# Paged samples: score before weighing, key gathers in groups of four, keys transposed by head pair

## The reference, cut to what matters

```
z      = q . k / 8 + bias[head]
log_1m = log_sigmoid(-z)                       # softplus(z), negated
rest   = sum of log_1m over all keys later than k
a      = exp(log_sigmoid(z) + rest)
out    = sum over k of a * v
```

## Time and profile before

| | us |
|---|---|
| median of three runs | 3324.55 |
| lowest, highest | 3321.88, 3334.59 |
| the profiled execution | 3332.23 |
| its span in the trace | 3330.1 |
| 32 steps of the changed stage, first exp to last exp | 1922.1 to 2677.0 |

### The profile page before, as it was taken

One profiled execution on the slowest core, in us unless ns is written; L12 is line 12 of the kernel. 1 busy time (PEld: TensorE's weight loads), 2 busy tenths in 40 slices (PEclk: granted clock), 3 DMA queues, 4 the chain that ended last, 5 costly groups with the idle time before them and its releaser, 6 DMA issues. The chain is left out here.

```text
span 3330.1 us, 47096 instructions
## 1 busy us (share of the span) xinstructions
PE 2939.2 (88%) x17542; PEld 2124.0 (64%) x17542; DVE 1658.2 (50%) x2730; ACT 1477.5 (44%) x2578; POOL 620.7 (19%) x908
## 2 busy tenths in 40 slices
PE   7999999998999999989999477777777765699998
PEld 5888768886555555558888354445445432388887
DVE  2000042223888888876666344445444434666663
ACT  4122131112777777765565244444444422433332
POOL 0000011111222222211133432232332300000000
PEclk9999999998999999999999688888888887799999
DMA  6665765555000001033223588888888866433321
GB/s 198 216 206 201 221 226 189 195 180 198 14 18 28 26 1 35 11 93 82 61 65 86 195 338 344 328 345 354 326 346 344 327 247 253 145 107 116 107 81 40
DMA packets 209765, 574.13 MB, mean 172 GB/s; under 512 B 40096, under 2 KB 109184, under 8 KB 173728
## 3 DMA queue, kind: packets, MB, share of 16 engines
q0 software_dynamic: 45568, 348.22, 27.4%
q1 hardware_dynamic: 164000, 223.27, 20.6%
HBM read 494.67 MB, written 143.73 MB: 192 GB/s over the span
## 5 line engine op out<-in xcount | busy, mean ns | idle before, releaser
L1570 DVE COPY sbs_kT<-sbs_ps_T 128x512 f32<-128x512 f32 x256 | 273.6, 1091 | 403.4 <-PE sbs_ps_T L1732 329.2
L495 PE MATMUL proj_ps_G<-proj_w_hi,proj_xT_hi 128*128 128x512 f32 x1024 | 399.8, 390 | 1.6 <-DVE proj_xT_lo L352 1.6
L499 PE MATMUL proj_ps_G<-proj_w_hi,proj_xT_lo 128*128 128x512 f32 x1024 | 398.6, 389 | 0.0
L497 PE MATMUL proj_ps_G<-proj_w_lo,proj_xT_hi 128*128 128x512 f32 x1024 | 398.5, 389 | 0.0
L1732 PE MATMUL sbs_ps_T<-held,sbs_k_ring 128*128 128x128 f32 x2048 | 319.2, 315 | 62.2 <-ACT sbs_kT L1653 30.1
L1732 PEld LDWEIGHTS sbs_ps_T<-held,sbs_k_ring 128*128 128x128 f32 x2048 | 281.3, 167 | 109.5 <-issue 53.7
L434 ACT ACTIVATE proj_out<-proj_ps_G,proj_stat 128x512 f32<-128x512 f32 (+1 forms) x136 | 93.4, 688 | 579.7 <-PE proj_ps_G L499 574.8
L1653 ACT ACTIVATE sbs_kT<-sbs_ps_T 128x512 f32<-128x512 f32 x256 | 271.0, 1102 | 102.3 <-PE sbs_ps_T L1732 84.6
L703 POOL CAST sbp_sp_hi<-sbp_sp 128x512 fp32r<-128x512 f32 (+3 forms) x320 | 171.9, 551 | 483.6 <-DVE sbp_sp L751 483.5
L751 DVE SCALAR_TENSOR_TENSOR sbp_sp<-sbp_Z,sbp_el 128x512 f32<-128x512 f32 (+3 forms) x320 | 180.6, 606 | 116.0 <-ACT sbp_el L833 116.0
L495 PEld LDWEIGHTS proj_ps_G<-proj_w_hi,proj_xT_hi 128*128 128x128 f32 x1024 | 192.3, 188 | 41.2 <-DVE proj_xT_lo L352 1.8
(11 more groups left out here) (295 smaller groups left out, 5811.1 us busy)
## 6 DMA issues: line engine op xcount, KB each, us to landing
out_k_win_s<-in_cache_k_win POOLq DMA_DIRECT2D x16, 2044.0 KB
out_v_win_s<-in_cache_v_win POOLq DMA_DIRECT2D x16, 2044.0 KB
dls_k_in<-in_cache_k_win SPq DMA_DIRECT2D x16, 1024.0 KB, 10.6
dls_v_in<-in_cache_v_win SPq DMA_DIRECT2D x16, 1024.0 KB, 14.5
proj_out<-in_w_in SPq DMA_DIRECT2D x28, 512.0 KB, 5.0
merge_o<-scratch_o_dil SPq DMA_DIRECT2D x48, 256.0 KB, 4.8
proj_x_in<-in_x_prompt SPq DMA_DIRECT2D x16, 512.0 KB, 4.3
scratch_xT_hi<-proj_xT_hi SPq DMA_DIRECT2D x16, 512.0 KB, 4.8
```

What stands on the lines that cost most here:

```text
L495: nc.tensor.matmul(ps_G[0:n, g, :], xT_hi[:, slot, k, 0:n], w_hi[:, k, cols], start=(k == 0), stop=False)
L497: nc.tensor.matmul(ps_G[0:n, g, :], xT_hi[:, slot, k, 0:n], w_lo[:, k, cols], start=False, stop=False)
L499: mm = nc.tensor.matmul(ps_G[0:n, g, :], xT_lo[:, slot, k, 0:n], w_hi[:, k, cols], start=False, stop=(k == KC - 1))
L1570: nc.vector.tensor_copy(by_lane(kT[:, j, :, :])[:, :, i, :], ps_T[:, x % TB, :].rearrange("p (a n) -> p a n", a=PAIRS)).then_inc(kT_odd, 1)
```

## The change

Three edits in `stick_breaking_sample`:

1. POOL asks for the four K chunks of a step, then for the four V chunks of the step before, instead of one of each in turn. The conditions are the same for each chunk, except that the wait for `av_done` stands once ahead of four V asks.
2. On TensorE `score(n+1)` comes before `weigh(n)`.
3. A unit of transposing is no longer a page but a pair of heads of a chunk: four transposes, one for each token position g of a row, write with a step of four elements (16 bytes) into one PSUM bank, so that the bank holds 512 keys in order, and the copy to `kT` is contiguous on both sides. The number of transposes, of copies and of signals is unchanged, and so is the order on DVE and ACT.

```diff
-            for q in range(NC * N + NC):
-                if q < NC * N:
-                    if q >= RING:
-                        pool.wait_ge(k_turned, GP * (q - RING + 1))
-                    gather(q, t["cache_k_sb"], k_ring, k_loaded)
-                if q >= NC:
-                    if q - NC >= RING:
-                        pool.wait_ge(av_done, (q - NC - RING) // NC + 1)
-                    gather(q - NC, t["cache_v_sb"], v_ring, v_loaded)
+            for n in range(N + 1):
+                if n < N:
+                    for q in range(NC * n, NC * n + NC):
+                        if q >= RING:
+                            pool.wait_ge(k_turned, GP * (q - RING + 1))
+                        gather(q, t["cache_k_sb"], k_ring, k_loaded)
+                if n > 0:
+                    if n > 2:
+                        pool.wait_ge(av_done, n - 2)
+                    for q in range(NC * n - NC, NC * n):
+                        gather(q, t["cache_v_sb"], v_ring, v_loaded)
...
-                nc.vector.tensor_copy(by_lane(kT[:, j, :, :])[:, :, i, :],
-                                      ps_T[:, x % TB, :].rearrange("p (a n) -> p a n", a=PAIRS)).then_inc(kT_odd, 1)
+                nc.vector.tensor_copy(kT[:, j, i, :], ps_T[:, x % TB, :]).then_inc(kT_odd, 1)
...
-                nc.scalar.activation(by_lane(kT[:, j, :, :])[:, :, i, :],
-                                     ps_T[:, x % TB, :].rearrange("p (a n) -> p a n", a=PAIRS), ACT.Copy).then_inc(kT_even, 1)
+                nc.scalar.activation(kT[:, j, i, :], ps_T[:, x % TB, :], ACT.Copy).then_inc(kT_even, 1)
...
-                for pr in range(PAIRS):
-                    tr = nc.tensor.transpose(ps_T[:, x % TB, pr * P:(pr + 1) * P], k_ring[:, q % RING, i, pr * P:(pr + 1) * P],
-                                             ident[:, :])
+                by_lane = ps_T[:, x % TB, :].rearrange("p (n g) -> p g n", g=GP)
+                for g_in in range(GP):
+                    tr = nc.tensor.transpose(by_lane[:, g_in, :], k_ring[:, q % RING, g_in, i * P:(i + 1) * P], ident[:, :])
                 tr.then_inc(k_turned, 1)
...
                 if n >= NSB and n % NSB == 0:
                     pick_rows(n // NSB - 1)
+                if nxt:
+                    score(n + 1)
                 if n >= 0:
                     weigh(n)
-                if nxt:
-                    score(n + 1)
```

More of the change, by code:

```diff
@@ L1478, in stick_breaking_sample @@
         block = ctx.enter_context(nc.Block())
-        def by_lane(keys):
-            return keys.rearrange("p a (n g) -> p a g n", g=GP)
         @block.sync
@@ L1563, in _, with copy_pair @@
             dve.wait_ge(n_copied, 2)
-            def copy_page(n, x):
+            def copy_pair(n, x):
                 j, i, g = x // GP, x % GP, SPP * n + x
@@ L1614, in _ @@
                 if nxt:
-                    copy_page(n + 1, 1)
+                    copy_pair(n + 1, 1)
                 if n >= 0:
@@ L1620, in _ @@
                 if nxt:
-                    copy_page(n + 1, 3)
+                    copy_pair(n + 1, 3)
                 if n >= 0:
@@ L1624, in _ @@
                 if nxt:
-                    copy_page(n + 1, 5)
+                    copy_pair(n + 1, 5)
                 if n >= 0:
@@ L1628, in _ @@
                 if nxt:
-                    copy_page(n + 1, 7)
+                    copy_pair(n + 1, 7)
                 if n >= 0:
@@ L1633, in _ @@
                     for x in (9, 11, 13, 15):
-                        copy_page(n + 1, x)
+                        copy_pair(n + 1, x)
             mask(DEC_B - 1)
@@ L1684, in _ @@
                 if nxt:
-                    copy_page(n + 1, 0)
+                    copy_pair(n + 1, 0)
                 if n >= 0:
@@ L1723, in _, with turn_pair @@
             pe.wait_ge(n_copied, 2)
-            def turn_page(n, x):
+            def turn_pair(n, x):
                 j, i, g, q = x // GP, x % GP, SPP * n + x, NC * n + x // GP
@@ L1790, in _ @@
                     for x in range(8):
-                        turn_page(n + 1, x)
+                        turn_pair(n + 1, x)
                 if n >= 0:
```

## The result

| | median us (range) | runs |
|---|---|---|
| kernel before, same chip | 3326.57 (3321.88 to 3334.59) | 4 |
| changed kernel | 3177.59 (3174.59 to 3184.67) | 4 |
| ratio | 0.9549, 95% interval 0.9525 to 0.9573 | |

The change takes off 149 us, more than three times the 45 forecast. The profiled execution has a span of 3182.5 us.

The account below looks back on a forecast made before the run. It took TensorE's signals, held up by gathers, as the bound, then DMA. Scan end 11.0 to 11.7 plus 11.5 gave a 22.9 us step against 24.35: -1.45 x 31 = -45 us, so 3280 us; range 3190 to 3370.

Parts of the forecast that it names:

- What bounds the kernel: Changed stage, 24.35 us a step: TensorE's signals held up during gathers; DMA second limit at 19.8 us.
- The law: Page copies ahead of the scan: a run of gathers holds up TensorE's signals until 2.0 to 2.7 us after its last gather.
- rival 1: Ahead of the scan: four asks leave signals alone, DMA becomes the bound; 126 to 141 us less, about 3190; chance 0.15.
- Rest of the step: From scan end to next exp: 14.1 us, less 3.46 for weighing, plus 0.9 for uncovered copies, is 11.5.
- The last sentence of the prediction: Behind the scan: if TensorE's clock stays at 1.00, not 0.63, another 1.5 to 2 us a step would go.
- Copies: PSUM to `kT`: contiguous copies take 0.60 us on ACT, 0.67 on DVE; -0.4 us each ahead of scan and scoring.
- Stepped PSUM writes at nothing: TensorE's transposes writing PSUM with a step of 16 bytes: extra cost taken as 0; upper bound 0.275 us a transpose.
- rival 2: TensorE's transposes: the stepped PSUM write costs time, up to 2.9 us a step, total about 3415; chance 0.22.
- Score ahead of weighing: TensorE's order: weighing's 3.46 us only move ahead of page 0; scoring then waits 0.9 us for the last copies.
- Rival 3: POOL's asks: K asks join the V asks, five or six in a run, gain cancels; 3305 to 3365, likeliest 3325; chance 0.18.

Follow-up runs that it names:

- the fours alone: Kernel before with only POOL's asks changed to four K chunks, then four V chunks; 3242.25 us, ratio 0.9725 on chip 5, where signals are late.
- set 4: Chip 5, against the kernel before (3333.36 us): whole change 3194.89, only asks by four 3242.25, only stepped transposes with contiguous copies 3326.31.
- the pairs: Kernel before with two edits, chip 9: asks by four plus contiguous copies 3177.96 us, 1.0001; asks by four plus scoring ahead of weighing 3211.00, 1.0113.

## Why the prediction was wrong, point by point

- *What bounds the kernel.* Right for the chip of the trace: late signals of TensorE, then DMA as the second limit at 19.8 us a step (8.39 MB at the 420 GB/s measured where it ruled are 20.0, with steps of 19.5 to 19.9).
- *The law, the failed step:* "By the law page 5's copy starts 2.0 to 2.7 after 7.2: at 9.2 to 9.9." It started at 6.82. The last of the held signals did come as the law says: the six asks' last one starts at 2204.11 and page 9's copy comes 2.33 us later. What was wrong is that every signal of a run is held until then. The prediction's own rows say otherwise: page 3's copy (2342.90) starts 0.89 us ahead of the last gather (2343.79), and pages 0 and 1 were on time, which I named for rival 1. Signals get through while the run goes on, the early ones at once and each later one later. In the changed kernel the first 24 transposes (pages 0 to 5) started 0.36 us ahead of the run and were over within 3 us of its start (2197.54 + 2.84), and page 5's signal passed. In the trace before, the run had begun 3.2 us ahead of the exp, so the same pages came further into it. I had written that down ("starts together with page 0 instead of 3.2 us ahead of it") and gave it no price. The term: scan end 11.35 forecast, 8.64 measured, -2.7 us a step.
- *Rest of the step.* Forecast 11.5 from scan end to exp, measured 10.85 (2202.88 to 2213.73). The wait for the last copies was 0.83 (forecast 0.9), and 1.3 us of held signals still stand in it. What got shorter is TensorE's own time: offset 0.52, pages 8 to 11 3.30, weights 0.59, pages 12 to 15 1.91, where the step of rows 3 has 0.93, 3.45, 0.85 and 2.27 (that step is 0.54 longer than the mean from which the forecast starts). The last sentence of the prediction had warned of the clock, and over the stage it rose to 0.99; but in the step shown pages 8 to 11 still ran at 0.57 (2203 to 2207), and only the last group was at 1.00. -0.65 us a step. Together 3.35 x 31 = 104 us, and 3280 - 104 = 3176. So the forecast missed by one large term, the hold-up ahead of the scan, and by a smaller one, TensorE's own time behind it.
- *Copies.* Right: 0.59 and 0.69 us. Alone they brought 0.2% where signals are late and nothing elsewhere.
- *Stepped PSUM writes at nothing (rival 2).* Right: the last group of 16 takes (1.91 - 0.27) / 15 = 0.109 us a transpose, where contiguous writes took 0.11. The Trainium skill ("Advanced Engine Details and Errata", PSUM Cachelines) has non-contiguous access slow matmuls significantly; for float32 transposes of 128 columns with a step of 16 bytes the trace shows nothing of it.
- *Score ahead of weighing.* Right that it only moves 3.46 us and uncovers the last copies; its price with stepped copies (1.08 us) was measured. What it brings, a run of gathers that starts with page 0 and behind the scores' signal, had no price in the sum. It was not measured alone where signals are late.
- *Rival 1.* Its time (3190) was nearest, its chance 0.15 too low. Its mechanism holds in half, so that its time was near is in part luck: page 5 is on time, and DMA is at 1.01. But no weighing waits for DMA in this trace; at 420 GB/s a step of 19.57 us brings 8.22 of the 8.39 MB, so by this estimate 31 steps used up 5.3 MB that the rings (16.8 MB) held ahead. The chain and DMA are now within 2% of each other.
- *Rival 3.* Its premise was right (the K asks of two chunks join, six in a run), its consequence not, for the same reason as the law.

What stays open: why TensorE's signals are late during a run of gathers, and why on some chips only. How the 47 us that the changed kernel gains over the fours alone (set 4) divide between scoring first and the copies is open too, as the pairs ran on a chip without late signals; the exps of the fours alone waited 33 us for the scores' signal, some 31 more than before. No version beat the changed kernel where signals are late.

## What to carry to other kernels

When a wait is explained by something that happens beside it, read from when on it is late as well as until when: a law with only an end point mis-sizes every change that moves the start. Group the asks that wait for one late event and put them where no short dependence crosses their run. And time a kernel on more than one chip before reading a gain off the program: the same two kernels differed by 4.2 to 4.5% on some chips and by 0.2% on another.

## What the runs showed of the hardware

- Two kinds of chips for one program: the kernel before took 3178 to 3180 us on two chips (8 and 9) and 3327 to 3334 on the others (3, 5, 15, and in the result, for which the record names no chip). The step was 19.81 against 24.35 us with the same instructions. Only chip 9 was met twice, so whether the kind belongs to the chip for good is not shown.
- Where signals are late, the last held signal of the runs read here fits the number of asks in the run (asks 1.24 us apart), not the time of the last one alone. From the first ask to the copy that had been held: 8 asks 11.36 us (2335.10 to 2346.46, rows 6 and 4), 7 asks 10.00, 6 asks 8.54 (2197.90 to 2206.44), 4 asks 5.73: 1.42 to 1.43 us an ask. It is a fit, not a cause.
- Before that end signals get through one by one. In the step of rows 3 to 6 the increments of pages 0 to 5, given 3.7 to 6.1 us after the first ask, took effect at 3.7, 4.2, 5.6, 7.8, 10.6 and 11.3. In the changed kernel those of pages 0 to 5 (given up to 2.5 us after it) were in time; the offset's, given 5.6 us after it, came 1.4 us late.
- No fixed time divides the two: with the fours alone, on chip 5, the scores' signal, given 3.1 us after the first ask, was 1.14 us late, and page 0's came only at the end of the run (5.73).
- Only TensorE's signals were late. In all 32 steps of the traces before and after, ACT's ln starts at most 0.04 us behind DVE's cut, and TensorE's offset at most 0.06 us behind DVE's scan.
- DMA gathered rows of 8 KB at 420 GB/s over 550 us.
